# A two-layer decoder trunk on eight cores: the second half of x asked for on another signal, two setup loads and the staged tiles behind a later one, one block of taps cut in two

## The reference, cut to what matters

```python
def conv_mixers(h, ...):                       # layer 0, mixers A and B
    z = h @ w_in
    a_val, a_gate, b_gate, c_gate, b_val = jnp.split(z, [...], axis=-1)
    a = a_val * jax.nn.sigmoid(a_gate)
    a = causal_depthwise_conv(a, conv_a_w) + conv_a_b          # 31 taps
    a = jax.nn.silu(layer_norm(a, ln_a_g, ln_a_b))
    bo = b_gate * causal_depthwise_conv(c_gate * b_val, conv_b_w)   # 3 taps
    return jnp.concatenate([a, bo], axis=-1) @ w_out

def chunked_spatial_gating(h, ...):            # layer 1, mixer C
    z = jax.nn.gelu(h @ w_in + b_in, approximate=False)
    u, v = jnp.split(z, 2, axis=-1)
    ...
    ws = jnp.where(mask[None], w_s, 0.0)       # 128x128, lower triangular, 8 groups
    sv = jnp.einsum("gts,bnsgc->bntgc", ws, vc) + b_s...
    return (u * sv) @ w_out

h = x
for i in range(2):
    h = h + mixer_i(rms_norm(h, g_i))
    h = h + squared_relu_mlp(rms_norm(h, mlp_norm_g[i]))
return rms_norm(h, final_norm_g)
```

## Time and profile before

| What | us |
|---|---|
| median of 3 timed runs | 2773.5 (2672.01, 2773.5 and 3225.67) |
| profiled execution, time | 2672.34 |
| profiled execution, span of the slowest core | 2670.7 |
| PE busy | 2633.8 (99% of the span) |
| first product of the kernel starts (L550) | 18.59 |
| second half of the first glu starts | 42.80 |

### The profile page before, as it was taken

One profiled execution on the slowest core, in us unless ns is written; L12 is line 12 of the kernel. 1 busy time (PEld: TensorE's weight loads), 2 busy tenths in 40 slices (PEclk: granted clock), 3 DMA queues, 4 the chain that ended last, 5 costly groups with the idle time before them and its releaser, 6 DMA issues.

```text
span 2670.7 us, 39681 instructions; the slowest of 8 cores (2667.2 to 2670.7 us)
## 1 busy us (share of the span) xinstructions
PE 2633.8 (99%) x13400; PEld 1260.6 (47%) x13400; DVE 1031.2 (39%) x1582; ACT 878.3 (33%) x1487; POOL 941.4 (35%) x1229
## 2 busy tenths in 40 slices
PE   6999999999999999999999999999999999999998
PEld 3544444455444444545544444444554444454443
DVE  3573213722443115643245212655233512274223
ACT  2434115432333235412234223532223421254112
POOL 3213233433533341403442433142344333325223
PEclk9999999999999999999999999999999999999999
DMA  9536344355575633454658544255555845326432
GB/s 198 119 62 121 64 79 78 66 99 99 109 189 114 125 64 64 75 94 89 108 109 229 95 95 88 40 95 101 89 103 105 207 75 91 68 39 106 78 64 79
DMA packets 57908, 265.28 MB, mean 99 GB/s; under 512 B 8176, under 2 KB 16368, under 8 KB 33904
## 3 DMA queue, kind: packets, MB, share of 16 engines
q0 software_dynamic: 29664, 202.39, 44.0%
q1 hardware_dynamic: 28048, 60.37, 7.2%
HBM read 439.67 MB, written 17.04 MB: 171 GB/s over the span
## 4 chain that ended last, share of the span: by engine, by line
PE 96%; SPq 1%; DMA 1%; POOL 0%; DVE 0%; issue 0%; ACT 0%; DVEq 0%; POOLq 0%; ACTq 0%
PE bank L550 91%; PE bank L431 2%; PE bank L795 2%; SPq L719 1%; PE bank L1020 1%; DMA h<-x 0%; DMA arena<-x 0%; POOL ring L356 0%; DMA ws_scr<-arena 0%; PE bank L832 0%; DVE arena L761 0%; POOL st L410 0%; ACT arena L804 0%; DVE xnT L434 0%; SPq L650 0%
## 5 line engine op out<-in xcount | busy, mean ns | idle before, releaser
L550 PE MATMUL bank<-xnT,ring 128*128 128x512 bf16 x5888 | 1294.2, 380 | 4.6 <-DVE xnT L434 3.1
L550 PE MATMUL bank<-ring,arena 128*128 128x512 bf16 x5120 | 1122.9, 379 | 0.0
L572 DVE TENSOR_TENSOR h<-bank,h 128x512 f32<-128x512 f32 x640 | 439.8, 691 | 1296.7 <-PE bank L550 1257.2
L550 PEld LDWEIGHTS bank<-xnT,ring 128*128 128x128 bf16 x5888 | 573.5, 98 | 681.5 <-issue 13.2
L550 PEld LDWEIGHTS bank<-ring,arena 128*128 128x128 bf16 x5120 | 498.4, 98 | 586.7
L600 POOL TENSOR_TENSOR arena<-arena 128x512 bf16<-128x512 f32 x512 | 551.1, 1082 | 310.3 <-ACT arena L598 310.2
L598 ACT ACTIVATE arena<-bank 128x512 f32<-128x512 f32 x512 | 303.6, 597 | 970.0 <-PE bank L550 928.3
L351 POOL DMA_DIRECT2D ring<-w x128 | 72.4, 567 | 453.8 <-PE bank L550 452.8
L406 ACT ACTIVATE junk<-h 128x1024 bf16<-128x1024 f32 x135 | 142.1, 1052 | 187.7 <-DVE h L572 178.8
L434 DVE TENSOR_TENSOR xnT<-bank,sm 128x1024 bf16<-128x1024 bf16 x128 | 155.0, 1216 | 51.4 <-PE bank L431 51.3
L408 POOL TENSOR_SCALAR st<-st 128x1 f32<-128x1 f32 x159 | 36.1, 227 | 380.0 <-ACT junk L406 378.4
(11 more groups left out here) (82 smaller groups left out, 997.0 us busy)
## 6 DMA issues: line engine op xcount, KB each, us to landing
ring<-w POOLq DMA_DIRECT2D x128, 1024.0 KB, 10.7
arena<-convw POOLq DMA_DIRECT2D x16, 1152.0 KB, 12.1
h<-x SPq DMA_DIRECT2D x32, 512.0 KB, 7.3
ring<-od_w_in POOLq DMA_DIRECT2D x16, 1024.0 KB, 10.1
y<-arena SPq DMA_DIRECT2D x31, 512.0 KB, 5.0
arena<-x SPq DMA_DIRECT2D x24, 512.0 KB, 11.0
ring<-ev_w_in POOLq DMA_DIRECT2D x10, 1024.0 KB, 16.2
ring<-ev_w_out POOLq DMA_DIRECT2D x8, 1024.0 KB, 12.1
```

Of the source, the lines that this page charges most:

```text
L550: r = e.matmul(banks[b][:], lhsT=lhs(kc), rhs=rhs(kc), start=start and n == 0, stop=stop and n == len(kcs) - 1)
L572: op("dve", lambda e: e.tensor_tensor(out=h[:, tb, d * 512:(d + 1) * 512], in0=banks[b][:], in1=h[:, tb, d * 512:(d + 1) * 512], op=ALU.ad ...
```

## The change

Four things change, and nothing of the arithmetic does.

1. Tiles 4 to 7 of x wait on SP for tile 3 of x, no longer for the first quarters of weight slots 0 and 1.
2. `prologue_loads` (`ws_f` and `bs_bc`, 512 KB each) moves from directly behind tiles 4 to 7 to behind the third gate, ahead of the first two staged tiles, which keep their place behind the same gate. `prologue_spatial` is called inside the table, behind `m0.to_x(1)`, where it also stood before.
3. The DMAs of `ws_scr` and `wsT_bf` get a semaphore of their own ("cs"), no longer the one of the small parameters ("c").
4. `b_taps` can be called in two parts (three instructions, then two), and `last_b` hands back: first taps, second taps, multiply 0, multiply 1 with the release of both held banks. It used to be: all taps, multiply 0, multiply 1, release.

```diff
         def prologue_loads():
             op("sp", lambda e: e.dma_start(out=ws_f, ...
-               [], [("ws_f",)], dma="cw")
+               [("aP", 2, 0)], [("ws_f",)], dma="cw")
...
-            op("sp", lambda e: e.dma_start(out=ws_scr, in_=ws_n), [("ws_n",)], [("ws_scr",)], dma="c")
+            op("sp", lambda e: e.dma_start(out=ws_scr, in_=ws_n), [("ws_n",)], [("ws_scr",)], dma="cs")
...
-            def b_taps(self, m):
+            def b_taps(self, m, parts=(0, 1)):
...
-                return [lambda: self.b_taps(3), lambda: self.b_mul(3, 0, bg[0]), lambda: self.b_mul(3, 1, bg[1]),
-                        lambda: held_banks.difference_update(bg)]
+                def last():
+                    self.b_mul(3, 1, bg[1])
+                    held_banks.difference_update(bg)
+                return [lambda: self.b_taps(3, (0,)), lambda: self.b_taps(3, (1,)), lambda: self.b_mul(3, 0, bg[0]), last]
...
                 for t in range(4, NTB):
-                    load_h(0, t, [("w", 0, 0), ("w", 1, 0)])
-                prologue_loads()
+                    load_h(0, t, h_keys(3))
...
-                3: [more_x(7), first_tr(7), more(3), lambda: pre.load(0, [("aP", 2, 0)]), lambda: pre.load(1)],
-                5: [lambda: m0.to_x(0)], 7: [lambda: m0.to_x(1)]}, {3: [first_tr(6)]})
-        prologue_spatial()
+                3: [more_x(7), first_tr(7), more(3), prologue_loads, lambda: pre.load(0), lambda: pre.load(1)],
+                5: [lambda: m0.to_x(0)], 7: [lambda: m0.to_x(1), prologue_spatial]}, {3: [first_tr(6)]})
...
-        m1.glu({0: [rest[0], lambda: m0.conv(2, 0)], 1: rest[1:] + [lambda: m0.conv(2, 1)],
-                2: [lambda: m0.conv(3, 0)], 3: [lambda: m0.conv(3, 1)],
+        m1.glu({0: [rest[0], lambda: m0.conv(2, 0)], 1: rest[1:3] + [lambda: m0.conv(2, 1)],
+                2: [rest[3], lambda: m0.conv(3, 0)], 3: [lambda: m0.conv(3, 1)],
```

More of the change, by code:

```diff
@@ L648, in prologue_spatial @@
             op("pool", lambda e: e.tensor_copy(out=ws_n, in_=ws_f.rearrange("p g t -> p (g t)")), [("ws_f",)], [("ws_n",)])
-            op("sp", lambda e: e.dma_start(out=ws_scr, in_=ws_n), [("ws_n",)], [("ws_scr",)], dma="c")
+            op("sp", lambda e: e.dma_start(out=ws_scr, in_=ws_n), [("ws_n",)], [("ws_scr",)], dma="cs")
             op("sp", lambda e, q: e.dma_start(out=wsT_bf[32 * q:32 * q + 32].rearrange("p g t -> p (g t)"),
                                               in_=ws_scr.rearrange("(n s) f -> s n f", s=4)[q]),
-               [("ws_scr",)], [("wsT_bf",)], dma="c", n=4)
+               [("ws_scr",)], [("wsT_bf",)], dma="cs", n=4)
             op("pool", lambda e: e.memset(ones_f, 1.0), [], [("ones_f",)])
@@ L756, in b_taps @@
                 o3 = self.cc
[L757 to L760, removed]
+                if 0 in parts:
+                    op("dve", lambda e: e.tensor_scalar(out=o3, in0=cg[:, :, 1:257], scalar1=wc(2), scalar2=None, op0=ALU.mult),
+                       allk + [("sm",)], [(cck,)])
+                taps = ((slice(1, 4), slice(0, 3), slice(1, 257), 1), (slice(0, 1), slice(3, 4), slice(0, 256), 1),
+                                      (slice(2, 4), slice(0, 2), slice(1, 257), 0), (slice(0, 2), slice(2, 4), slice(0, 256), 0))
+                for so, si, cs, t in (taps[:2] if 0 in parts else ()) + (taps[2:] if 1 in parts else ()):
                     op("dve", lambda e, so=so, si=si, cs=cs, t=t: e.scalar_tensor_tensor(
```

## The result

The changed kernel takes 2679.4 us, the median of 11 runs (2676.8 to 3093.3), against 2672.4, likewise of 11, for the kernel before; the ratio is 1.0025, with a 95% interval of 1.0014 to 1.0035. So it is some **6.7 us slower** (0.0025 x 2672), where 1.5 us less was forecast. The highest times belong to executions in which the cores of a die or of both ran some per cent longer at a lower clock; the ratio above and every ratio and median from here on are made without these (the changed kernel's median is then 2679.1).

A forecast was written before the change was run, and what follows sets the result against it. PE, busy 2633.8 of 2670.7 us, was taken to bound the kernel, leaving at most 36.9 us to win. The terms -1.95 + 0.5 = -1.45 against 2672.34 gave 2670.9 us (chance 0.45), range 2661 to 2680.

The forecast's parts named there:

- Taps in two parts: On DVE two taps and one multiply come later; PE waits for none, no bank changes hands: 0 us.
- rival C: SP's issues run faster, both later waits (3.9) go, clock at the front stays up (1.5): 2665.5; chance 0.15.
- The later MLPs: In the two MLPs where the tap list also hangs, PE waits for none of it: 0 us.
- The tiles: Front: x tiles 4 to 7 issued 3.1 us earlier, so third gate and second half come 1.95 us earlier.
- its signs: Expected in the trace: x issued 11.5, third gate 31.3, second half 41.3 (wrong if after 42), `to_x` 50.6.
- The weights: Front: earlier x slows sva's m = 2 quarter, landing 29.4, wanted 28.9: PE waits 0.5 us.
- The other quarters have more room by the same count: Front: weight quarters other than sva's m = 2 have more room; no wait was counted for them.
- Setup loads and "cs": `ws_f`, `bs_bc` and staged tiles come later, the semaphore is separate: nobody waits, 0 each.
- SP's chain: From `to_x` (52.13) to staged tiles 2 and 3; PE's waits of 1.5 and 2.4 stay: 0 us.
- If it shifts as PE does: Condition on SP's chain, which starts with the second half's second gate: both later waits then stay, 0 us.
- A: Slower: queue 0 slow throughout, sva's third quarter 3.1 us late, decided by a wait above 1.95: 2673.5; chance 0.15.
- B: No gain: SP's chain doesn't shift, or tiles 4 to 7 land no earlier: 2672.3; chance 0.25.

The follow-up runs named there:

- e7: Kernel before with the second multiply and bank release one step later in the first macro tile only, taps whole; 2675.95 against 2672.2 us, ratio 1.0013.
- e4: Changed kernel, DVE's order kept, both banks held one step longer so PE's fourth gate starts on bank 3; 2673.7 against 2672.4 us, ratio 1.0007.
- e1: Kernel before with only the taps in two parts, the new `last_b` list and `m1.glu` table; 2678.4 against 2672.4 us, ratio 1.0025.
- e3: Changed kernel, taps still split, second multiply and release back behind the second gate in the first MLP; 2674.2 against 2672.4 us, ratio 1.0007.
- e2: Changed kernel with the taps part taken back, so only loads and semaphore differ from before; 2672.85 against 2672.4 us, ratio 1.0003.
- e11: Kernel before with tiles 4 to 7 of x issued at once behind tile 3, without any wait; 2674.1 against 2672.3 us, ratio 1.0020.
- e12: Kernel before with tiles 4 to 7 of x and the setup loads issued later, behind the m = 1 weight quarters; 2674.4 us, ratio 0.9999.
- e6: Kernel before with setup loads, staged tiles and "cs" moved as in the change, x and taps as before; 2672.4 against 2672.2 us, ratio 0.9995.
- e9: Kernel before with ACT's statistics of staged tiles 2 and 3 behind the first convolution copies, their scaling behind `b_branch(2)`; 2669.8 against 2672.3 us, ratio 0.9985.
- e10: e6 with the same ACT reordering as e9; 2669.4 us, ratio 0.9981 to the kernel before.

## Why the prediction was wrong

The sign was wrong, by a part that I had put at nothing. Its terms in turn.

**Taps in two parts: 0. Here the sum failed**, with the step "PE waits for none of these ... and no bank changes hands". That the banks are the same is true, and it was the wrong question. I read PE's order for the bank numbers and DVE's for what moved, and did not put the two together: bank 1's reader had moved behind four sums, a gate product and a copy, and PE takes bank 1 as soon as it is through with the convolution. The rows for it were in the trace of before: the multiplies end at 132.55 and PE wants the bank at 134.16, a margin of 1.6 us. Put ahead of the second multiply are four sums, 2.34, a gate product, 0.68, and a copy, 1.21: 4.2 us, less the margin a wait of 2.6. That is what e7 has, 2.2 to 2.8; the taps' second half, which the split also puts behind a gate product, adds what is left to 3.3. e4 shows the bank to be the cause and not DVE's order. Of the loss, e1 holds 6.0 us. The changed kernel less e4 is 5.4 us (2679.1 - 2673.7): 2.2 to 3.3 of wait, and 1.5 to 2.7 of lower clock on seven of the cores. The clock's fall stood nowhere in my sum; only rival C spoke of the clock, at the front.

**The later MLPs: 0.** Wrong by the same step. The bank's reader ends 0.35 us late in each; e3 and e4, which keep these waits, are 1.3 and 0.9 above e2, of which the waits seen are 0.7. The rest is inside the noise.

**The tiles: -1.95.** The mechanism is right: ACT's wait of 2.48 and PE's of 1.91 are gone where the tiles come early (ACT has at most 0.6 left, on two cores of the changed kernel). The rest of its signs did not come with it: x was issued at 11.8 (11.5 forecast), but the third gate is at 33.60 (31.3), the second half at 43.56 (41.3, and wrong from 42 on) and `to_x` at 53.1 (50.6).

**The weights: +0.5.** The landing was right, 29.4 forecast and 14.2 + 15.5 = 29.7 measured. The time at which it is wanted was wrong, and that is the second step that failed: "PE wants it eight products (1.7 us) before 30.59, at 28.9". Both quarters of m = 2 count on one semaphore, and PE waits for the count of both ahead of the sixteen products. The rows of PE's order, of the second and the third gate, with the semaphores waited for:

```
L550 MATMUL bank<-xnT,ring 128x512 [waits d_wa1_0]
L550 MATMUL bank<-xnT,ring 128x512 x15
L550 MATMUL bank<-xnT,ring 128x512 [waits d_wa2_0]
L550 MATMUL bank<-xnT,ring 128x512 x15
```

So sva's quarter is wanted sixteen products before 30.59, at 30.59 - 16 x 0.226 (3.61 by 16) = 27.0. With that the wait is 29.4 - 27.0 = 2.4 and the front -1.95 + 2.4 = +0.45, as e2's time has it. The agreement is closer than it deserves, since the wait differs by core from 1.0 to 3.1 and the mean start of the second half moved by 0.8 in the changed kernel and by 1.9 in e2. Nor was that quarter the only one: "The other quarters have more room by the same count" failed too. Of the 1.9 us of waits in the mean of the changed kernel's cores, 1.1 are for m = 2 and 0.8 for m = 3 (3.06 on core 1), a term that the sum did not have. What is shown is that both terms are there and nearly cancel, and that the kernel before sits near the best point: e11 loses by weights, e12 by tiles, some 2 us each.

The Trainium skill, "DMA: Bandwidth & Descriptors", section "Queues, rings and completion order", has each DMA engine take turns between queues with work, a packet at a time, where its packet is a bundle of descriptors. In the changed kernel queue 0 got 163 packets and queue 1 166 in 18 to 22, which agrees. The onset does not. Core 7 issues x from 11.8, and in 11.8 to 15.2 its DMA view has queue 0 alone (packets, MB, share):

```profile
q0 software_dynamic: 238, 0.43, 100.7%
```

So the silence of queue 1 behind its issue, in the earlier trace rows from 14.57 to 18, came again with the earlier issue. On this core the sharing began between 15 and 16, where the prediction had put it at 14.9 and the rule at 11.5, and the landing came within 0.3 us of the count.

**Setup loads and "cs": 0 and 0.** Right: e6. e9 adds that ACT, when it has nothing else to wait for, does wait for the semaphore "c", but e10 is only 0.4 us below e9, so even then "cs" is worth nothing that could be measured.

**SP's chain: 0, the two later waits stay.** Half right. Both stay on core 0 of the changed kernel (1.2 and 2.4), as on two other cores; two keep only the second, and three have neither. Before, it was much the same: four cores with both, two with the second alone and two with neither. "If it shifts as PE does" failed where PE moved far: in e11 PE is 4.7 us later and the staged tile 0.9. I treated the two waits as a fixed cost behind the front; they are a cushion that takes up part of a delay, as e11 shows on all its cores. A front whose second half starts 1.9 us later costs 0.45 (e2), and by the same reason one that came earlier might give less than it gains, which no run here tried.

**The rivals.** A, late weights, is what the front did: the wait for them, 1.9 us in the mean of the changed kernel's cores, stands at A's turning point of 1.95, and on one core of e2 the waits add up to 4.7. A's 2673.5 is 0.65 above e2. B's first half, that SP's chain keeps its time when PE moves, is nearer to what e11 shows than my own step; B's number was near e2's too, but its terms were others. C did not happen; it was right that the two later waits can go, but they went by ACT's order (e9: 2.5 us); its lighter queue did not show, `to_x` takes 24.4 us in the mean of the changed kernel's cores against 25.1 before, where C wanted up to 5 us. No rival spoke of the second multiply. The range, 2661 to 2680, held the time only because it had been widened for another execution and chip. That it would stay within 2% held as well, but 2% is not the grain of such a measurement: the interval of the result is 0.2% wide.

What stays open: why the lower clock comes behind a wait of 3.28 on some cores and not on others (e1: five of eight), and with that 1.5 to 2.7 us of the loss by core and execution; and what sets the time of SP's chain, which moved less than PE.

## What to carry to other kernels

When an instruction that reads a bank is moved, the bank's next writer must be looked up and the time between the two compared with what was put in between; that the banks keep their numbers says nothing. For a DMA wait, read which transfers count on the semaphore before saying when one of them is wanted. A wait later on the same chain takes up a delay as readily as it eats a gain, so price a front edit only after asking what the next wait on that chain hangs on, and look whether that one can be taken away by itself.

## What the hardware showed

The lower clock doesn't follow from the length of a wait alone. Behind waits of 2.2 to 3.3 us on the same bank the first products ran at 1.2 GHz on seven of eight cores in the changed kernel, five of eight in e1 (three with a wait of 3.28 kept 2.4 GHz, their sixteen products taking 3.61 us) and one of eight in e7. In the changed kernel it came behind both waits of 2.23 and not behind the one of 2.61. Where it comes it costs 1.3 us (e7) to 2.7, most often 1.7, half of a wait of 3.3 again.

The second queue's start depends on who was first. With x issued at once (e11) core 3's DMA view of 10 to 14 has (packets, MB, share of 16 engines):

```profile
q1 hardware_dynamic: 304, 1.10, 88.0%
q0 software_dynamic: 18, 0.04, 5.6%
```

The weights, issued meanwhile, got 18 packets; in the earlier trace rows and in the changed kernel it was x that got none for over three microseconds behind its issue. In e11, four microseconds later, the two shared, 190 to 188. No run here says what the late one waits for.
